# A's projection in a hybrid decoder step: third to eighth tile as three pairs of seven block products, weights of the output projection in the same ring, middle chunk stored by two tiles

## The reference

```python
h = rms_norm(x, g_norm[l]) * (1 + scale) + shift
proj = h @ w_in[l]
y_a, nc = conv_branch(proj[..., :o1], proj[..., o1:o2], proj[..., o2:o3], ..., w_a_out[l])
y_b, npl = pool_branch(proj[..., o3:o4], proj[..., o4:o5], ..., w_grp[l], pool_scale[l], w_b_out[l])
m = jax.nn.sigmoid(proj[..., o5:o6]) * y_a + jax.nn.sigmoid(proj[..., o6:]) * y_b
x = x + gate * (m @ w_out[l])
return rms_norm(x, g_final), ...
```

## Time and profile before

| | before |
|---|---|
| median of 3 runs | 919.88 us |
| lowest, highest | 919.63, 924.82 us |
| profiled execution | 920.5 us |
| its span, first to last instruction | 918.7 us |
| granted TensorE clock, mean | 0.995 |
| PE busy | 903.2 us (98%) |
| DVE busy | 797.1 us (87%) |
| ACT busy | 414.4 us (45%) |

### The profile page before, as it was taken

One profiled execution on the slowest core, in us unless ns is written; L12 is line 12 of the kernel. 1 busy time (PEld: TensorE's weight loads), 2 busy tenths in 40 slices (PEclk: granted clock), 3 DMA queues, 4 the chain that ended last, 5 costly groups with the idle time before them and its releaser, 6 DMA issues.

```text
span 918.7 us, 17120 instructions
## 1 busy us (share of the span) xinstructions
PE 903.2 (98%) x7004; PEld 885.0 (96%) x7004; DVE 797.1 (87%) x913; ACT 414.4 (45%) x582; POOL 100.7 (11%) x109
## 2 busy tenths in 40 slices
PE   8999999999999999999999999999999999999995
PEld 5699999999999999999999999999999989999995
DVE  1797999997999995999996899999798797689767
ACT  5484354434453443454443454446444432526452
POOL 0121211111020211211111203000011000000000
PEclk9999999999999999999999999999999999999998
DMA  9979989889688979698988989648987672423515
GB/s 365 349 190 211 254 209 241 240 228 247 190 230 246 254 241 239 190 249 239 288 219 257 231 221 221 211 134 288 368 331 176 215 247 90 142 70 113 163 48 184
DMA packets 86334, 202.75 MB, mean 221 GB/s; under 512 B 12401, under 2 KB 19057, under 8 KB 82801
## 3 DMA queue, kind: packets, MB, share of 16 engines
q1 hardware_dynamic: 52928, 122.76, 39.0%
q0 software_dynamic: 22080, 52.46, 28.1%
q10 hardware_dynamic: 11248, 26.45, 8.2%
HBM read 175.67 MB, written 88.88 MB: 288 GB/s over the span
## 4 chain that ended last, share of the span: by engine, by line
PE 95%; DMA 2%; DVE 1%; SPq 1%; issue 0%; ACT 0%; DVEq 0%
PE ps L1080 23%; PE ps L1076 23%; PE ps L1074 23%; PE ps L1011 8%; PE ps L1014 8%; PE ps L1012 8%; DMA ada_raw<-w_ada 2%; PE ps L941 1%; PE ps L993 1%; PE ps L947 0%; DVE hf L2374 0%; PE ps L1272 0%; PE ps L1270 0%; PE ps L1269 0%; DVE bf L1821 0%; PE ps L954 0%
## 5 line engine op out<-in xcount | busy, mean ns | idle before, releaser
L2012 DVE SCALAR_TENSOR_TENSOR conv_y<-conv_u,par_all,conv_y 128x1024 f32<-128x1024 f32 x240 | 300.8, 1281 | 2.1 <-DVE conv_y L1998 0.6
L1076 PE MATMUL ps<-tr,hr 128*128 128x258 f32 x824 | 216.3, 283 | 0.0
L1074 PE MATMUL ps<-tr,hr 128*128 128x258 f32 x824 | 215.4, 283 | 0.0
L1466 ACT ACTIVATE hr<-raw 128x512 fp32r<-128x512 f32 (+1 forms) x188 | 115.9, 618 | 115.3 <-PE ps L1080 87.5
L1080 PE MATMUL ps<-tr,hr 128*128 128x258 f32 x824 | 166.3, 283 | 0.0
L1076 PE MATMUL ps<-hr 128*128 128x258 f32 x616 | 161.4, 283 | 0.0
L1074 PE MATMUL ps<-hr 128*128 128x258 f32 x616 | 160.8, 282 | 0.0
L1074 PEld LDWEIGHTS ps<-tr,hr 128*128 128x128 f32 x824 | 156.9, 190 | 0.1
L1076 PEld LDWEIGHTS ps<-tr,hr 128*128 128x128 f32 x824 | 155.6, 189 | 0.0
L1891 DVE TENSOR_TENSOR hr<-raw,hr 128x512 fp32r<-128x512 f32 (+1 forms) x188 | 126.1, 675 | 4.6 <-ACT hr L1466 0.7
L1080 PEld LDWEIGHTS ps<-tr,hr 128*128 128x128 f32 x824 | 127.2, 188 | 0.0
(11 more groups left out here) (289 smaller groups left out, 1580.9 us busy)
## 6 DMA issues: line engine op xcount, KB each, us to landing
w_sums<-w_main POOLq DMA_DIRECT2D x64, 512.0 KB, 9.5
raw<-w_sums SPq DMA_DIRECT2D x120, 256.0 KB, 4.4
raw<-w_main SPq DMA_DIRECT2D x94, 256.0 KB, 4.5
w_sums<-w_sums POOLq DMA_DIRECT2D x30, 512.0 KB, 5.4
w_sums<-w_main ACTq DMA_DIRECT2D x26, 512.0 KB, 5.6
ada_raw<-w_ada SPq DMA_DIRECT2D x8, 1024.0 KB, 21.0
w_raw<-w_main SPq DMA_DIRECT2D x16, 512.0 KB, 5.9
bf<-x_t SPq DMA_DIRECT2D x4, 1032.0 KB, 8.2
```

The costliest lines, as they stand in the source:

```text
L1074: nc.tensor.matmul(bank[:, c, :], wh[:, w_cols], x_hi[:, k, t_cols], start=start and k == 0, stop=False, skip_group_check=True)
L1076: nc.tensor.matmul(bank[:, c, :], wh[:, w_cols], x_lo[:, k, t_cols], start=False, stop=False, skip_group_check=True)
L1466: nc.scalar.activation(ring(q)[0][:, 0:n], raw5[:, raw_slot(q), 0:n], ACT.Copy).then_inc(item_hi, 1)
L2012: ins = v.scalar_tensor_tensor(out=y, in0=conv_u[:, x, k:k + SEQ], scalar=par_all[:, g, x, k:k + 1], in1=y, op0=ALU.mult, op1=ALU.add)
```

## The change

1. a's tiles 0 and 1 stay plain; the other six are three pairs A_A (2, 3), A_B (4, 5), A_C (6, 7), 21 block products in a new order. The order in which m is done becomes 0, 1, 3, 2, 5, 4, 7, 6. The pairs of a use the same banks as those of out.
2. One ring of four slots, `RING`, runs from the first block of A_A to the last: a's 21 blocks, the weights of out's tiles 0 and 1 as half tiles (W0, W1), out's 14 blocks, and half tiles for out's tiles 7 and 6. The loads into `w_raw` and their splits of 128x1024 for these are gone.
3. POOL sums the weights of one pair more: a chunk of A_C and OUT_A, and one of OUT_B alone.
4. The middle chunk of the result is stored in four parts of two tiles in place of two of four; one part is normed ahead of the sum of squares and of `last_x(2, 1)`.

```diff
-PLAIN_A = 3
-JOB_A_LAST = JOB_A + PLAIN_A
-JOB_OUT = JOB_A_LAST + 1
+PLAIN_A = 2
+JOB_OUT = JOB_A + PLAIN_A
...
-A_ITEMS = [("P1", A_A), ("P1", A_B), ("P6", A_A), ("P2", A_A), ("P7", A_A), ("P5", A_A), ("P6", A_B), ("P4", A_A), ("P3", A_A),
-           ("P2", A_B), ("P7", A_B), ("P5", A_B), ("P4", A_B), ("P3", A_B)]
+A_ITEMS = [("P1", A_A), ("P1", A_B), ("P5", A_A), ("P2", A_A), ("P6", A_A), ("P2", A_B), ("P7", A_A), ("P6", A_B), ("P4", A_A), ("P3", A_A),
+           ("P7", A_B), ("P1", A_C), ("P5", A_B), ("P4", A_B), ("P3", A_B), ("P6", A_C), ("P5", A_C), ("P7", A_C), ("P2", A_C),
+           ("P4", A_C), ("P3", A_C)]
...
+RING = A_ITEMS + [("W0", 0), ("W1", 0), ("W0", 1), ("W1", 1)] + OUT_ITEMS + [("W0", 7), ("W1", 7), ("W0", 6), ("W1", 6)]
...
-OUT_PARTS = [(0, 0, 4), (0, 4, KT), (1, 0, 4), (1, 4, KT), (2, 0, 2), (2, 2, 4), (2, 4, 6), (2, 6, KT)]
+OUT_PARTS = [(0, 0, 4), (0, 4, KT)] + [(c, m, m + 2) for c in (1, 2) for m in range(0, KT, 2)]
...
             split_for(JOB_B + 7)
+            first_sums(OUT_B // 2)
...
             merge_a(0, JOB_A)
-            split_for(JOB_A)
+            item_lo_part(A_SPLIT)
+            item_lo_part(A_SPLIT + 1)
             link(v.tensor_tensor(full22, br[:, upper_k, second].bitcast(F32), hr[:, upper_k, second].bitcast(F32), ALU.add))
             link(v.scalar_tensor_tensor(out=at2, in0=at1, scalar=-1.0, in1=full22, op0=ALU.mult, op1=ALU.subtract))
             dve.sem_inc(t_summed, 1)
+            a_t_lo("P5", 1)
             merge_a(1, JOB_A + 1)
...
+            def plain_out(m, order):
+                for j, k in enumerate(order):
+                    if j % KH == 0:
+                        pe.wait_ge(item_lo, A_SPLIT + RING_AT["W0" if k < KH else "W1", m] + 1)
+                    pe.wait_ge(m_lo_done, M_ORDER.index(k) + 1)
+                    last = ring_step(m, k, m_hi[k], m_lo[k], j == 0, j == KT - 1)
+                    if j % KH == KH - 1:
+                        last.then_inc(item_done, 1)
...
             second_rstd = row_inverse(1)
+            norm(second_rstd)
             last_sum(2, [0])
             last_x(2, 1)
+            norm(second_rstd)
             norm(second_rstd)
             inverse(2)
             norm(second_rstd)
```

More of the change, by code:

```diff
@@ L811, in _ @@
[L811 to L834 removed]
+            load_block(17)
@@ L836, in _ @@
+            sp.wait_ge(m_full, M_ORDER.index(2) + 1)
+            load_sig_a(6)
+            for i in range(18, OUT_RING - 2):
+                load_block(i)
+            sp.wait_ge(m_full, M_ORDER.index(5) + 1)
+            load_x(1)
             sp.wait_ge(m_full, M_ORDER.index(4) + 1)
             load_x(0)
-            load_main(JOB_OUT + 1)
-            sp.wait_ge(m_full, M_ORDER.index(5) + 1)
-            load_x(1)
-            for i in range(4):
-                load_out_item(i)
+            for i in range(OUT_RING - 2, OUT_RING + 4):
+                load_block(i)
@@ L846, in _ @@
             load_x(3)
-            for i in range(4, len(OUT_ITEMS)):
-                load_out_item(i)
+            for i in range(OUT_RING + 4, OUT_RING + len(OUT_ITEMS)):
+                load_block(i)
             sp.wait_ge(x_new_ready, 3)
@@ L866, in _, with sum_tiles @@
             sp.wait_ge(pool_state_stored, 32 * PAIRS)
-        def sum_inputs(c):
-            if c < N // 2:
-                first = FIRST_PAIR_BLOCK + 4 * c
-            else:
-                first = MAIN_B + KT + A_TILE[A_A] if c == A_A // 2 else MAIN_B + 2 * KT + OUT_TILE[OUT_A]
-            tiles0, tiles1 = (t["w_main"][first + x:first + 4:2].rearrange("a p c -> p a c") for x in range(2))
+        def sum_tiles(c):
+            if c < N // 2:
+                return FIRST_PAIR_BLOCK + 4 * c, 2, 2
+            if c == A_A // 2:
+                return MAIN_B + KT + A_TILE[A_A], 2, 2
+            if c == A_C // 2:
+                first = MAIN_B + KT + A_TILE[A_C]
+                return first, MAIN_B + 2 * KT + OUT_TILE[OUT_A] - first, 2
+            return MAIN_B + 2 * KT + OUT_TILE[OUT_B], 1, 1
+        def sum_inputs(c):
+            first, step, count = sum_tiles(c)
+            tiles0, tiles1 = (t["w_main"][first + x:first + x + step * (count - 1) + 1:step].rearrange("a p c -> p a c") for x in range(2))
             return tiles0[:, :, 0:FORM_COLS], tiles0[:, :, FORM_COLS:], tiles1[:, :, 0:FORM_COLS], tiles1[:, :, FORM_COLS:]
         def sum_output(c, n):
-            return t["w_sums"][2 * c:2 * c + 2, n].rearrange("a p c -> p a c")
+            return t["w_sums"][2 * c:2 * c + sum_tiles(c)[2], n].rearrange("a p c -> p a c")
         @block.gpsimd
@@ L1214, in gate_turn, with ring_step @@
                 modulation_turn(aux[:, n, :], gate_rows).then_inc(gate_turned, 1)
+            def ring_step(m, k, hi, lo, start, stop, chunks=range(CHUNKS)):
+                wh, wl = ring(A_SPLIT + RING_AT["W0" if k < KH else "W1", m])
+                w_cols = slice(k % KH * P, (k % KH + 1) * P)
+                for c in chunks:
+                    out = ps[:, m % 2, c, 0:CW]
+                    nc.tensor.matmul(out, wh[:, w_cols], hi[:, cols(c)], start=start, stop=False)
+                    nc.tensor.matmul(out, wh[:, w_cols], lo[:, cols(c)], start=False, stop=False)
+                for c in chunks:
+                    last = nc.tensor.matmul(ps[:, m % 2, c, 0:CW], wl[:, w_cols], hi[:, cols(c)], start=False, stop=stop)
+                return last
             single(JOB_A, a_hi, a_lo, before_k=lambda k: pe.wait_ge(a_lo_done, k + 1))
@@ L2151, in a_result @@
                 first, second = HALVES
-                if form not in ("P2", "P5", "P4", "P3"):
+                c22 = i == max(A_AT["P5", n], A_AT["P7", n])
+                if form not in ("P2", "P4", "P3") and not c22:
                     return
@@ L2205, in _ @@
             dve.sem_inc(t_summed, 1)
[L2206 to L2209 removed]
             for n in range(2):
                 gate_modulation(n)
[L2212 to L2216 removed]
+            link(v.scalar_tensor_tensor(out=at4, in0=at2, scalar=-1.0, in1=br[:, upper_k, first].bitcast(F32), op0=ALU.mult, op1=ALU.subtract))
@@ new lines, in _ @@
+                if (form, n) == ("P2", A_B):
+                    a_t_lo("P4", 4)
+                if (form, n) == ("P5", A_C):
+                    m_split_lo(0)
+                if (form, n) == ("P7", A_C):
+                    m_split_lo(1)
+                if (form, n) == ("P2", A_C):
+                    m_split_lo(3)
+                if (form, n) == ("P4", A_C):
+                    for m in (2, 5, 4):
+                        m_split_lo(m)
+            m_split_lo(7)
+            m_split_lo(6)
```

348 lines of the change are left out of this document (132 added, 216 removed).

## The result

| | before | after |
|---|---|---|
| median, 21 runs each | 920.30 us | 921.96 us |
| lowest, highest | 919.51, 924.82 us | 920.60, 924.35 us |
| ratio of the times, 95% interval | | 1.0021 (1.0014 to 1.0028) |
| profiled execution, its span | 920.5, 918.7 us | 922.16, 920.4 us |

The account below looks back on a forecast made before the run. PE, busy 98% of the span, was taken as the bound. Terms -2.6 + 2.7 + 1.2 - 0.8 = +0.5 on the profiled 920.5 gave 921.0, and the median, 0.6 lower, 920.4 us; range 917.8 to 922.9.

Parts of the forecast that it names:

- PE's work: Two plain tiles of a replaced by seven more block products: PE has 2.6 us less to do.
- The first wait: Start of the pairs, before P2 of the second pair: PE waits about 2.7 us for C11's read and the seed.
- the rival of no wait: Start of the pairs: DVE some 3 us quicker than walked, C11 out by 769.8, time 916.5; chance 0.12.
- The second wait: Hand-over to the output projection: PE waits about 1.2 us before P1 of OUT_B for plain_x(1), bounds 0.5 to 2.0.
- The end: Last stores: one 344 KB part leaves early, late parts start about 0.5 later; net -0.8 us, bounds -1.0 and +0.5.
- my bandwidth sum: Last stores: a 0.35 MB part leaving before the full stretch, at 0.36, is worth 0.98 us.
- weights through the ring cost nothing of their own: Weights loaded through the ring instead of w_raw: smaller splits under PE's work, same columns read by out's products, no cost.
- loads at nothing: Block loads and the added POOL sums: in time, no cost; a load 3 us later would show only there.
- The clock rival: PE's clock falls in the wait at the start of the pairs, costing 1.65 us: 922.1; chance 0.12.
- The rule on large transfers: Last stores: the skill wants at least 1 MiB per transfer; by it the end's 0.8 us gain would be nothing.
- The DVE backlog rival: Hand-over to the output projection: DVE's backlog a microsecond or two longer, PE waits more, 921.5 to 924.5; chance 0.16.

## Why the prediction was right, and where it was not

The time lies in the stated range (921.96 in 917.8 to 922.9), and "no difference of 1%" came out. It lies 1.6 above the point forecast of 920.4, though, and above the 919.3 to 921.6 that had the chance of 0.60. The two waits were right in mechanism and size; the end was right in neither: it was worth more than the 0.8 forecast, and a load that the prediction had at nothing took it all back. That the sum still ends in the range is partly luck. Step by step:

- **PE's work, -2.6.** 124.70 - 127.21 = -2.51 without waits. Right.
- **The first wait, 2.7.** Measured 2.85, with C11 at 771.91 (walked: 771.8) and the seed behind it. The walk down DVE's order was right within 0.1 us over 29 us. Shown by the run with C11 first: -2.91. The point that decides the rival of no wait, C11 out by 769.8, is met in that run (768.21 + 0.69), and there PE does not wait.
- **The second wait, 1.2.** Measured 1.18. `plain_x(0)` started at 833.79 (833.5) and `plain_x(1)` at 844.45 (844.1). Right; that the backlog goes on behind it, with the next step 0.5 us short as soon as this one is mended, I had not seen ("behind this point DVE has pauses again").
- **The end, -0.8.** Sized too small, and then lost to something else. The late parts started at 28.23 as said. The new end by itself is worth more: 1.14 by the medians, 1.45 in the traces (36.37 - 34.92), beyond my bound of -1.0. The early part is 0.8 of it by the run with the norms behind last_x, near the 0.98 of my bandwidth sum. The rest, the halving by itself, I had at nothing; the traces give it 0.7 (36.36 - 35.69), the medians nothing (919.88 against 920.07), so it stays open. A small slip beside it: the 3% between 355 and 366 GB/s are 0.06 us for each of the two parts that are halved, 0.12 in all.
- **The step that failed** is "weights through the ring cost nothing of their own", with "loads at nothing". I had counted the columns that PE reads and the loads of weights, and not the loads of PE's own program, which grew by 24 matmuls and their weight loads. The 56th block of it fell among the last stores and took 1.4 us in the profiled execution (36.36 - 34.92), so that -1.45 became 0. The sum by measured terms: -2.5 + 2.85 + 1.18 = 1.5, 1.65 in the trace, and nothing from the end: +1.65, against +1.66 in the medians (1.3 to 2.6 by the interval of the ratio, so that the second digit is chance).
- **The clock rival.** It came true in part. In the changed kernel's own profile the granted clock is 1.00 from 31.9 to 912.5 us, over the idle time of 2.85. But with the old end the clock fell behind the same wait for 3.4 us, and with fewer matmuls of ones for 6.8; the stretch of the pairs grew by 1.5 and 2.7 us, where one such fall was priced at 1.65. Mechanism and price of the rival are right, and 0.12 looks too low: it came in two of four profiled executions. How often it comes in the 21 runs of the changed kernel isn't known. The warning of the Trainium skill, "TensorE: Matmul & The Clock Gate", Why this matters for your kernels, was borne out in these two and not in the other two.
- **The rule on large transfers** (the Trainium skill, "DMA: Bandwidth & Descriptors", Rules for kernel authors, with its 1 MiB per transfer). By it the new end would have won nothing; the kernel before with 344 KB parts and one of them early was 1.14 faster, and with 344 KB parts alone no slower. When the bytes may leave counts here more than the size of the parts.
- **The DVE backlog rival** was not needed; the second wait was as forecast.

What stays open: the medians put the changed kernel's cost with the old end at 3.0 us (1.8 to 5), the traces at 1.65 plus 1.3 for the packet. That fits, but the lower clock behind the first wait costs 1.5 in one of these traces and is in neither sum, so the share of each in the medians isn't settled. The packet's share when it falls behind the end was not measured by itself, and what moves it there in the same program isn't known.

## What to carry to other kernels

Walk the order of the engine that feeds the bound one, instruction by instruction with durations from the trace: it gave both waits here within 0.2 us, and tells which two instructions to swap. A wait ahead of dense work can cost more than its own length, because the clock can be lower behind it; price that too. When such an engine has no slack, a mended wait moves to its next instruction, so read on until the first pause. And at the end of a kernel, where only stores are left, count every packet that shares the DMA engines, the program's own too; one execution's end is not the kernel's end, so compare the same stretch in several before a term of a microsecond is believed.

## What the runs showed of the hardware

- With a 16 KB packet of PE's instructions among the last stores they landed in 3.6 us where it was 2.7 without, and the end came 1.4 us later (36.36 against 34.92, by the same program on PE). A few instructions more in a program, even behind the last needed one, moved it (29.2 and 16.4 us behind the start of the last two tiles); in two kernels with the same program on PE it stood at 28.9 and 36.2.
- Behind PE's idle time of 2.7 us between dense block products the granted clock was at 0.50 for 3.4 us in one execution and 6.8 in another, and stayed at 1.00 in two. Behind 1.0 us alone it stayed at 1.00 in three of three.
- The same eight matmuls of 86 columns took 1.09 us at the full granted clock and up to 1.98 at the lower level, and what waits for them came up to 0.7 us later. The clock fell there in some executions with the same work ahead of them (three kernels), and in all three kernels in which two matmuls of ones ahead of them were dropped, at least in part.
- At the start the eight matmuls took 1.09 us each time up to 20 us in one execution and 0.64 from 8.2 us on in another, with 10 and 28 matmuls ahead of them. The profile holds no record of the clock before it first reaches its full level (26.4 and 8.0 us), and a stretch without a record reads 1.00: durations are the surer sign there.
